# Five modulation rows through DRAM in place of ScalarE spreads and TensorE products

## The reference

```python
def first_block(x, c, ...):
    c_act = jax.nn.silu(c)
    mod = (c_act @ ada_w[i] + ada_b[i])[:, None, :]
    sh1, sc1, g1, sh2, sc2, g2 = jnp.split(mod, 6, axis=-1)
    h = rmsnorm(x, mix_norm_pre[i]) * (1.0 + sc1) + sh1
    y = windowed_gqa_sink(h, ...)
    x = x + g1 * rmsnorm(y, mix_norm_post[i])
    h = rmsnorm(x, ffn_norm_pre[i]) * (1.0 + sc2) + sh2
    y = swiglu(h, ffn_w_in[i], ffn_w_out[i])
    x = x + g2 * rmsnorm(y, ffn_norm_post[i])

def second_block(...):                      # for each of the two layers i
        sh1, sc1, g1, sh2, sc2, g2 = ...silu_c @ ada_w[i] + ada_b[i]
        hx = modulate(xs, sh1, sc1)         # h * (1.0 + scale) + shift
        yx = mixer_ab(hx, hc, ...) if even else mixer_pool(hx, ...)
        xs = layer_norm(alpha * xs + g1 * yx, ln_g[i, 0], ln_b[i, 0])
        hx = modulate(xs, sh2, sc2)
        fx = peer(hx, peer_wq[i], peer_keys[i], peer_u[i], peer_v[i])
        xs = layer_norm(alpha * xs + g2 * fx, ln_g[i, 1], ln_b[i, 1])
```

## Time and profile before

| | us |
|---|---|
| Runs | 2071.8, 2074.97, 2075.92 (median 2074.97) |
| Profiled execution | 2070.76, of which the trace spans 2069.0 |
| PE busy | 1744.1 (84%) |
| DVE busy | 1469.1 (71%) |
| ACT busy | 919.5 (44%) |
| POOL busy | 613.1 (30%) |
| SP (issues only) | no busy time listed |
| Transfers | 723.24 MB in 114,651 packets, mean 350 GB/s |

### The profile page before, as it was taken

The page is one execution under the profiler, slowest core; times in us unless marked ns, Lnnn a source line. Parts: engine busy times, 40 slices in busy tenths (PEclk is TensorE's granted clock), DMA queues, the critical chain, the costliest instruction groups (busy, mean ns, idle before and its releaser), DMA issues.

```text
span 2069.0 us, 21998 instructions
## 1 busy us (share of the span) xinstructions
PE 1744.1 (84%) x6989; PEld 1026.8 (50%) x6989; DVE 1469.1 (71%) x3271; ACT 919.5 (44%) x2397; POOL 613.1 (30%) x575
## 2 busy tenths in 40 slices
PE   3888999899888798987887787998999978778876
PEld 2657998788767354533322323464555423223322
DVE  6778877888876587766677767527776767667675
ACT  3555444444472344453444444334444444444443
POOL 1250000000002354433434343114455433433431
PEclk9998999999999999999999999999999999999999
DMA  9654768566645999999999999859999999999996
GB/s 380 267 193 182 265 245 305 215 256 243 242 166 205 418 421 422 421 421 417 421 421 422 421 421 421 325 188 384 408 418 421 421 422 421 422 421 421 422 421 256
DMA packets 114651, 723.24 MB, mean 350 GB/s; under 512 B 11484, under 2 KB 13300, under 8 KB 34024
## 3 DMA queue, kind: packets, MB, share of 16 engines
q0 software_dynamic: 75152, 541.35, 63.1%
q1 hardware_dynamic: 39384, 180.50, 23.5%
HBM read 720.72 MB, written 1.08 MB: 349 GB/s over the span
## 4 chain that ended last, share of the span: by engine, by line
DMA 38%; PE 30%; DVE 18%; ACT 7%; issue 4%; POOL 3%; SPq 0%; ACTq 0%; DVEq 0%
DMA X<-in_k_uv,EI 24%; DMA Z<-in_k_uv,EI 12%; PE PS L2266 12%; PE PS L1956 4%; PE PS L1958 4%; PE PS L1957 4%; DVE junk L1943 3%; DVE W L1568 3%; PE PS L2242 3%; DVE WL L1580 2%; POOL X L1074 2%; ACT WH L1083 1%; PE PS L2283 1%; ACT L1083 1%; ACT E L1083 1%
## 5 line engine op out<-in xcount | busy, mean ns | idle before, releaser
L2266 PE MATMUL PS<-X,dg 128*128 128x512 f32 x1380 | 666.7, 616 | 129.2 <-ACT dg L1083 128.5
L1943 DVE CUSTOM_DVE_ANT_0 junk<-H,X 128x1024 f32<-128x1024 f32 x345 | 421.9, 1223 | 240.6 <-DMA X<-in_k_uv,EI 235.9
L1074 POOL DMA_INDIRECT X<-in_k_uv,EI x345 | 364.8, 1057 | 512.5 <-PE PS L2266 378.1
L2266 PEld LDWEIGHTS PS<-X,dg 128*128 128x128 f32 x1380 | 249.2, 193 | 504.7 <-ACT dg L1083 289.1
L1083 ACT ACTIVATE CF<-DOT 128x1 f32<-128x1 f32 x512 | 103.6, 202 | 661.2 <-DVE DOT L1943 660.3
L2266 PE MATMUL PS<-Z,dg 128*128 128x512 f32 x480 | 237.6, 622 | 56.4 <-ACT dg L1083 55.9
L1943 DVE CUSTOM_DVE_ANT_0 junk<-H,Z 128x1024 f32<-128x1024 f32 x120 | 146.8, 1223 | 95.6 <-DMA Z<-in_k_uv,EI 93.8
L1083 ACT ACTIVATE dg<-CP,CG 128x128 f32<-128x128 f32 x512 | 205.5, 401 | 18.2 <-PE PS L2266 1.5
L1956 PE MATMUL PS<-XH,WH 128*128 128x256 f32 x592 | 174.5, 295 | 16.2 <-DVE XL L1483 14.8
L2266 PEld LDWEIGHTS PS<-Z,dg 128*128 128x128 f32 x480 | 84.5, 192 | 189.9 <-ACT dg L1083 123.2
L1957 PE MATMUL PS<-XL,WH 128*128 128x256 f32 x592 | 170.5, 288 | 0.0
(11 more groups left out here) (319 smaller groups left out, 2509.6 us busy)
## 6 DMA issues: line engine op xcount, KB each, us to landing
W<-in_k_ada SPq DMA_DIRECT2D x58, 1024.0 KB, 5.4
W<-in_k_win SPq DMA_DIRECT2D x15, 1024.0 KB, 5.7
Y<-in_k_ada SPq DMA_DIRECT2D x14, 1024.0 KB, 6.3
W<-in_k_ffi SPq DMA_DIRECT2D x14, 1024.0 KB, 5.5
Y<-in_k_ffi SPq DMA_DIRECT2D x8, 1024.0 KB, 6.6
W<-in_peer_wq SPq DMA_DIRECT2D x8, 1024.0 KB, 14.0
W<-in_ffn_w_out SPq DMA_DIRECT2D x6, 1024.0 KB, 7.6
W<-in_ab_w_out SPq DMA_DIRECT2D x6, 1024.0 KB, 6.2
```

The source lines that it names most:

```text
L1074: e.indirect_dma_start(out=WS[k][:, :], out_offset=None, in_=I[f"k_uv{ly}"][:, :], in_offset=bass.IndirectOffsetOnAxis(ap=EI[t][:, j:j + 1 ...
L1943: e.tensor_tensor_reduce(junk, H[:, t, :], d[:, 0:D], 1.0, 0.0, ALU.mult, ALU.add, DOT[:, j:j + 1]).then_inc(v_dot, 1)
L2266: p = e.matmul(PS[:, 2 * t + q, :], dgb[n % 4][:, :], d[:, D + q * 512:D + (q + 1) * 512], start=(j == 0), stop=(j == 127))
```

## The change

For rows 0 to 4, the three steps become two, both on GpSimd's queue. `roww` writes the column from the tile `MC` to a small tensor `rows` in DRAM: 128 x 8 values whose places in DRAM are 512 bytes apart within a partition, so each goes as a single value of 4 bytes, 1,024 of them for a row. `rowr` reads the row's 4 KB back to all 128 partitions, 512 KB in the tile, once the write is complete (`d_rw`), and raises `d_row`. 40 products on TensorE (10 groups of four) and 15 instructions on ScalarE go. The 1.0 that `rowv` added to sc2 is now added once by VectorE, in the step `mod 8`, to the column itself, with a wait for its own result before it; `sc` no longer adds it for layer 0. Rows 5 to 9 are made as before, with their counters renumbered.

`rowr` waits for the row before it and, for rows 2 to 4, for the tile to be free: row 2 for `post(0)` (`v_add`), rows 3 and 4 for TensorE's last score transposes (`p_dt`). In the plan, row 0's steps now stand at attention unit 18, row 1's at FFN output part 2 behind `gc 1`, the writes of rows 2 to 4 and the read of row 2 at step 6 of the differential attention, and the reads of rows 3 and 4 after the last `turn_head`, directly followed by `fold` and `sc`.

```diff
-        if n >= 19:
-            row(0, n - 19, 1)
+        if n == 18:
+            P("roww", 0)
+            P("rowr", 0)
...
             P("mod", 4)
             P("gc", 1)
-        if 3 <= i < 6:
-            row(1, i - 3, 3)
+            P("roww", 1)
+            P("rowr", 1)
...
-            if n in (6, 7, 8) and k == 4:
-                row(2, n - 6, 5)
+            if (n, k) == (6, 4):
+                for r in (2, 3, 4):
+                    P("roww", r)
+                P("rowr", 2)
             if (n, k) in gates:
                 P("gate", gates[n, k], k % 2)
-            if (n, k) == (17, 0):
-                P("rowv", 3)
-            if n == 17 and k in (2, 4):
-                row(3, k // 2, k // 2 - 1)
...
     turn_head(7, 3)
-    P("rowv", 4)
-    next(g)
-    row(4, 1, 0)
-    next(g)
-    row(4, 2, 1)
-    next(g)
+    P("rowr", 3)
+    P("rowr", 4)
     P("fold", 0)
     P("sc", 0)
...
+        row_d = nc.dram_tensor("rows", [5, D], F32, kind="Internal")
...
                         w.wait_ge(v_add, 4)
                         w.wait_ge(p_do, 16)
-                        w.wait_ge(p_row, 10)
+                        w.wait_ge(v_lam, 2)
...
+                elif kind == "roww":
+                    r = a[0]
+                    if r < 2:
+                        w.wait_ge(v_gc, r + 1)
+                    else:
+                        w.wait_ge(v_mod, nth("mod", 8))
+                    e.dma_start(bass.AP(row_d, r * D, [[1, 128], [128, 8]]), ROWS[r][0],
+                                allow_slow_non_contiguous=True).then_inc(d_rw, 16)
+                elif kind == "rowr":
+                    r = a[0]
+                    w.wait_ge(d_rw, 16 * (r + 1) if r < 2 else 80)
+                    if r:
+                        w.wait_ge(d_row, 16 * min(r, 3))
+                    if r == 2:
+                        w.wait_ge(v_add, 2)
+                    elif r > 2:
+                        w.wait_ge(p_dt, 16)
+                    e.dma_start(ROWS[r][1][:, :], spread(row_d[r:r + 1, :])).then_inc(d_row, 16)
...
-                    w.wait_ge(a_row, 10 if ly == 0 else 18)
+                    if ly:
+                        w.wait_ge(a_row, 8)
+                    else:
+                        w.wait_ge(d_row, 80)
...
-                    w.wait_ge(a_row, 2 + 2 * r)
+                    w.wait_ge(d_row, 16 * (r + 1))
...
-                    e.tensor_tensor(dst, dst, bias, ALU.add).then_inc(v_mod, 1)
+                    q = e.tensor_tensor(dst, dst, bias, ALU.add)
+                    if s == 8:
+                        q.then_inc(v_own, 1)
+                        w.wait_ge(v_own, own.up())
+                        q = e.tensor_scalar(MC[1][:, 32:40], MC[1][:, 32:40], 1.0, None, ALU.add)
+                    q.then_inc(v_mod, 1)
```

More of the change, by code:

```diff
@@ L82, in xt @@
             P("xl", i, c)
-    def row(w, h, b):
-        if h == 0:
-            P("rowv", w)
-        else:
-            P("rowp", w, h - 1, b)
-            P("rowa", w, h - 1, b)
     low, first = (0, 1, 2), (0, 1, 2, 4, 5, 6, 7, 3)
@@ L814, in build @@
             "ctx", "lam", "gn", "r5", "r1", "k", "out", "c", "c2"))
-        d_slot = [sem(f"d_slot{k}") for k in range(len(WS))]
+        d_rw, d_row = sem("d_rw"), sem("d_row")
+        d_slot = {k: sem(f"d_slot{k}") for k in sorted({place[0] for name, place in where.items() if name[0] != "ga"})}
         d_gath = {k: sem(f"d_gath{k}") for k in RING}
@@ L994, in _ @@
                     e.dma_start(R[5][0:1, :], I["ln_g_2"][ly, 1:2, :]).then_inc(d_r5, 16)
-                    w.wait_ge(p_row, 18 if ly == 0 else 20)
+                    w.wait_ge(p_row, 8 if ly == 0 else 10)
                     e.dma_start(R[1][0:1, :], I["ln_b_2"][ly, 1:2, :]).then_inc(d_r1, 16)
@@ L1113, in _ @@
                         w.wait_ge(p_part, IN if r else FI)
-                    if r:
-                        w.wait_ge(p_row, 4)
                     for i in range(2):
@@ L1252, in _ @@
                     col, dst, via, plus = ROWS[r]
-                    if r < 2:
-                        w.wait_ge(v_gc, r + 1)
-                    else:
-                        w.wait_ge(v_mod, nth("mod", 8 if r < 6 else 11))
-                    if r == 1:
-                        w.wait_ge(a_sq, 8)
-                    elif r == 2:
-                        w.wait_ge(v_lam, 1)
-                    elif r == 5:
+                    w.wait_ge(v_mod, nth("mod", 8 if r < 6 else 11))
+                    if r == 5:
                         w.wait_ge(v_x, nth("x", 1))
@@ L1264, in _ @@
                         w.wait_ge(v_x, nth("x", 5))
-                    elif r:
-                        w.wait_ge(p_row, 2 * r)
+                    else:
+                        w.wait_ge(p_row, 2 * (r - 5))
                     act(heads(via), col.unsqueeze(2).to_broadcast([128, 8, 128]), ACT.Identity,
@@ L1270, in _ @@
                     r, q, b = a
-                    w.wait_ge(p_row, 2 * r + q + 1)
-                    if r == 1:
-                        w.wait_ge(a_row, 2)
-                    elif r == 2:
-                        w.wait_ge(v_add, 2)
-                    elif 3 <= r < 6:
+                    w.wait_ge(p_row, 2 * (r - 5) + q + 1)
+                    if r == 5:
                         w.wait_ge(p_dt, 16)
-                    elif 6 <= r < 9:
+                    elif r < 9:
                         w.wait_ge(v_h, 2)
-                    elif r == 9:
+                    else:
                         w.wait_ge(v_rn, nth.rn["brn", 1])
@@ L1774, in _ @@
                         w.wait_ge(a_tt, nth.tt_a["tt", 0, 1])
-                    e.tensor_scalar(M[:, 32:40], M[:, 32:40], 1.0, None, ALU.add).then_inc(v_own, 1)
-                    w.wait_ge(v_own, own.up())
+                    if ly:
+                        e.tensor_scalar(M[:, 32:40], M[:, 32:40], 1.0, None, ALU.add).then_inc(v_own, 1)
+                        w.wait_ge(v_own, own.up())
                     e.tensor_tensor(G2c2[:, 0:8], gcol, M[:, 32:40], ALU.mult)
@@ L1786, in _ @@
                         w.wait_ge(*arena(ly))
-                    w.wait_ge(a_row, 6 if ly == 0 else 14)
+                    w.wait_ge(*((a_row, 4) if ly else (d_row, 48)))
                     res_sum(("rn", ly, t), t, yb(t), R[0])
@@ L1796, in _ @@
                     t = a[0]
-                    w.wait_ge(a_row, 12)
+                    w.wait_ge(a_row, 2)
                     w.wait_ge(v_x, nth("x", t))
@@ L1802, in _ @@
                     t = a[0]
-                    w.wait_ge(a_row, 20)
+                    w.wait_ge(a_row, 10)
                     w.wait_ge(v_x, nth("x", 4 + t))
@@ L2142, in _ @@
                     via = ROWS[r][2]
-                    w.wait_ge(a_rv, r + 1)
+                    w.wait_ge(a_rv, r - 4)
                     take(b)
@@ L2148, in _ @@
                     p.then_inc(p_row, 1)
-                    free[b] = [(a_row, 2 * r + q + 1)]
+                    free[b] = [(a_row, 2 * (r - 5) + q + 1)]
                 elif kind == "lnp":
```

## The result

| | before | after |
|---|---|---|
| Median of the runs | 2075.44 (4 runs) | 2090.85 (4 runs) |
| Lowest and highest | 2071.8, 2076.07 | 2090.34, 2095.04 |
| Ratio | | 1.0082, 95% interval 1.0067 to 1.0097 |
| Span of the profiled execution | 2069.0 | 2088.5 |
| First gather at | 663.44 | 684.55 |

The prediction was 2071.5 with a range up to 2079.0. The time is 19 us above the first and 12 above the second. The loss is complete at the first gather (21.1 us in the traces) and nothing is added behind it: from the first gather to the end of the span, the trace of before takes 1405.6 us and that of after 1404.0.

The account below looks back on a forecast made before the run. PEER's transfers and gathers bound the later part, unchanged; before it, TensorE's products and VectorE's modulation products in turn. 0 − 1.60 + 0.18 − 0.43 − 1.60 = −3.45 us, so median 2071.5, range 2065.0 to 2079.0.

Parts of the forecast that it names:

- Row 0: Before `post(0)`: removed work hidden under VectorE, gain 0; write done at 147.05, row there about 2.3 us before `post`.
- Row 1: FFN output stage: TensorE leads, so −1.6 us; added transfers fall in free DMA time; upper end 0, the gain given back.
- Rows 2 to 4: Differential attention: three writes and a read beside weight loads, taken as 0; a load up to 4.8 us late, for the range.
- third rival: Single values are slow: at 0.16 us a piece row 0 comes 7.9 us late, giving 2079.4; chance 0.16.
- outer bound: At `post(0)`: row 0 comes 20.7 us late, giving 2092.2 us; left outside the range.
- Row 4's term: Products before the first residual: two TensorE groups of 0.80 us go, −1.6 us.
- Row 3's 0.43: At gate 3: VectorE's 0.43 us wait for TensorE goes, and no more than that can come forward.
- second rival: All hidden or given back: loads become the limit in row 1's stage, waits after row 4; 0 to +1, 2075; chance 0.17.
- The moved steps: Mixer's end: `rowr` 3 and 4, `fold`, the layer norm's loads and `sc` all hidden, cost 0.
- `mod 8`'s extra addition: At `mod 8`: the separate addition of 1.0 costs VectorE one small operation and its wait, +0.18 us.
- The two rules that were weighed: Fixed DMA cost about 2.0 us would bring row 0 some 7 us earlier; one descriptor per strided element underlies the third rival.

Follow-up runs that it names:

- e10_fill: The changed kernel with neither writes nor reads: GpSimd fills the tiles of rows 0 to 4 with 1.0; 2073.93 us, ratio 0.9992.
- e3_rows234: The kernel before with only rows 2, 3 and 4 through DRAM, fold and sc moved as in the change; 2083.90 us, ratio 1.0044.
- e9_tr_late: The change with each column transposed by one product, written as 8 pieces of 512 bytes, row 1's product at FFN output part 4; 2074.61 us, ratio 0.9992.
- e5_readonly: The changed kernel without the five writes; the five 512 KB broadcasts read a row of ln_g instead; 2075.83 us, ratio 1.0004.
- e4_pieces32: The changed kernel with each row written as 128 pieces of 32 bytes instead of 1,024 of 4, values permuted; 2075.10 us, ratio 0.9995.
- a0: The kernel before, instruction for instruction, run again as an experiment; 2074.29 us, ratio 0.9993.
- e1: The kernel before with only row 0 through DRAM as single values; 2079.63 us, ratio 1.0019.
- e2: The kernel before with only row 1 through DRAM; 2079.97 us, ratio 1.0027.
- e13: The kernel before plus five unused writes of 1,024 single values, 64 bytes apart, at the times of the change's writes; 2075.52 us, ratio 1.0002.
- e11_right32: The change with 32-byte pieces, made right: rows read through a view with a step of 8, four GpSimd copies before fold; 2080.70 us, ratio 1.0025.

## Why the prediction was wrong, step by step

**Row 0 ("nothing, if the row lands in time").** The mechanism was right and both durations too small: the write was done 4.2 us after my 147.05 (0.9 of it because GpSimd's last scaling ended later), and the read took 9.1 us in the median where I had taken 7.5 from an 8 KB broadcast. The wait was 1.96 in the trace. I had not priced what the transfers do to the load of `in_k_ada` next to them, and the whole row cost 4 us.

**Row 1 ("fall in the slack of a fifth").** This is the step that failed, and of which most can be learned. The products' part of it was right: −1.6 in the sum, 1.8 us in e10_fill. But I had counted the added write by its bytes, 4 KB, and given it the DMA share that was free. The engines moved 170 GB/s in place of 374 for 10 us; VectorE waited 7.5 us for a load, and row 1 alone made the kernel 4.2 us slower. The upper end I had kept for this step was "the gain of 1.6 is given back". It should have been a multiple of it.

**Rows 2 to 4 ("a load behind them could come up to 4.8 late, of which a load's slack takes a part").** The same step failed here. It was right in kind, at less than half the size: 9.96 us of waiting, and 0 in the sum, where e3_rows234 showed 8.1. This is the largest part of the loss. Three lists behind each other had been put at one list's spread.

**The bound of the third rival.** It was the right place to look, and its price per piece at 0.16 us gave 2079.4. But it priced only row 0's lateness, took the slow writes' effect on the loads as an afterthought, and got its end from 2,048 pieces of 512 bytes (`KK`). That row showed that pieces as such are cheap, which is true, and hid that these pieces aren't of that kind; `KK` is a load, too. That its outer bound, 2092.2, lies near the 2090.85 measured is chance: it came from a row 20.7 us late, and the row was 1.96 late. I had also read the 10.2 as a bound for any list of small pieces; for one that fills neighbouring places of 4 bytes from different partitions it is no bound.

**Rows 3 and 4, and where the gain goes.** Row 4's term (−1.6) is seen where I put it: from gate 3 to the first residual 20.9 and 20.2 us in the two traces of before, 19.0 and 18.8 in e10_fill and e9_tr_late, so 1.2 to 2.1 less. Row 3's 0.43 is too small to be told. But the gains don't reach the medians. One part is that two traces of the same program lie 4.3 us apart at the first gather (663.44 and 667.70), more than the whole sum. Another is that the stretch from 528 to 603, behind row 2's place, is 1.4 to 3.5 us longer in e10_fill and e9_tr_late than in the two of before, and 2.1 to 2.8 in e5_readonly and the change, though not in e4_pieces32 (75.27) and e3_rows234 (75.12). In the four longer ones ScalarE waits 2.9 to 4.4 us for a load of `in_k_win` there; in the six traces that make rows 2 to 4 as before, where the stretch is 74.9 to 75.9, it waits 1.6 to 3.2. The granted clock is 0.91 to 0.93 in the first and 0.91 to 0.95 in the others, so it doesn't tell them apart. That looks in part like my second rival, given back to loads, but no run tested it. Where the 3.4 us go stays open.

**The moved steps** cost nothing, as predicted: with e4_pieces32, which has all of them, the time is that of before. As it also lacks the products, a cost could hide behind their gain; but from the first residual to the first gather the traces with the moved steps (e3, e4, e5, e9 and e10) take 24.6 to 26.8 us, and those without (before, a0, e1, e2 and e13) 24.5 to 26.8. `mod 8`'s extra addition is too small to be seen.

**The two rules that were weighed.** The Trainium skill's rule against strided last dimensions (page "DMA: Bandwidth & Descriptors", "Rules for kernel authors") had the right sign for the write of the change. But what it names, one descriptor for each element, isn't what costs here: e13_spaced has as many elements, with as much of a stride, and costs nothing in place; on idle engines 1,024 spaced values took 3.2 to 3.7 us and 128 contiguous pieces 1.95. The Trainium skill's fixed cost of about 2.0 us (same page, "Anatomy of one DMA — SWDGE (gpsimd) path") fits the 1.8 to 1.95 us that 8 and 128 pieces took on idle engines, and is far from the 9 of single values next to each other. Here the measurements decide.

## What to carry to other kernels

A small write isn't priced by its bytes, and hardly by its number of pieces, but by where neighbouring partitions' pieces fall: keep single values 64 bytes apart (8 were enough on idle engines), or make each partition's piece 32 bytes. Pieces of 8 or 16 bytes side by side were not tried. And a transfer that nobody waits for can still be the most expensive one, since the loads that follow it slow down to a third: look at the GB/s of the stretch, not at the wait for the transfer. When products on a busy engine are to be removed, fill their result with a constant first and time that; here it would have shown that little or nothing of the gain reaches the median.

## What the runs showed of the hardware

- 1,024 writes of 4 bytes to DRAM take 9 to 10 us on idle engines when neighbouring partitions' values are 4 bytes apart, and 4.1 (0.88 + 3.23) when they are 8 bytes apart. It is a step, and it depends little on the number: 512, 1,024 and 2,048 values took about 9 to 11 us.
- While they complete, a stream of loads falls from 367 to 110 GB/s for 10 us; a load issued 0.2 to 0.3 us ahead of them landed after 4.9 and 6.3 us, alone after 4.8 and 5.0. What in the memory or the engines makes it so, no run here shows.
- Reading 1,024 single values back took 3.1 to 3.4 us on idle engines (a median of 2.9 from issue to landing), so it is a matter of writing.
- A product on a view with a step of 8 values took VectorE 2.11 us for two halves in place of 1.28 (e11_right32).
